# Where GpSimd waits at the entrances of the feed-forward parts and of the convolution mixer

## The reference

```python
def short_conv_mixer(h, norm_g, w_in, conv_w, w_out):
    xn = rms_norm_2(h, norm_g)
    proj = xn @ w_in
    gate_b = proj[..., :CONV_WIDTH]
    gate_c = proj[..., CONV_WIDTH:2 * CONV_WIDTH]
    u = proj[..., 2 * CONV_WIDTH:]
    y = gate_b * causal_dwconv(gate_c * u, conv_w)
    return y @ w_out

def conv_ffn_2(h, norm_g, w_up, conv_w, w_down):
    xn = rms_norm_2(h, norm_g)
    u = causal_dwconv(xn @ w_up, conv_w)
    g, val = u[..., :D_FF], u[..., D_FF:]
    return (jax.nn.silu(g) * val) @ w_down
```

## Time and profile before

| | |
|---|---|
| median of 3 runs | 1234.81 us (1234.18 to 1236.0) |
| profiled execution, its own time | 1238.09 us |
| profiled execution, span from first to last instruction | 1236.1 us |
| TensorE busy | 1224.3 us, 99% of the span |
| VectorE busy | 752.1 us, 61% |
| GpSimd busy | 712.6 us, 58% |
| ScalarE busy | 676.5 us, 55% |
| mean granted TensorE clock | 0.996 |

### The profile page before, as it was taken

One profiled execution on the slowest core, in us unless ns is written; L12 is line 12 of the kernel. 1 busy time (PEld: TensorE's weight loads), 2 busy tenths in 40 slices (PEclk: granted clock), 3 DMA queues, 4 the chain that ended last, 5 costly groups with the idle time before them and its releaser, 6 DMA issues.

```text
span 1236.1 us, 24028 instructions
## 1 busy us (share of the span) xinstructions
PE 1224.3 (99%) x8458; PEld 1090.7 (88%) x8458; DVE 752.1 (61%) x1660; ACT 676.5 (55%) x1226; POOL 712.6 (58%) x308
## 2 busy tenths in 40 slices
PE   8999999999999999999999999999999999999998
PEld 4788889877799999999988779999999989899998
DVE  5786667455641766655626654766667445766665
ACT  6343344454544755555755626666667556666663
POOL 5466553442168765557585305755565986755573
PEclk9999999999999999999999989999999999999999
DMA  9978552231135454456464203554554764555451
GB/s 338 374 251 301 202 160 84 84 104 52 52 115 177 154 204 183 174 197 210 130 205 137 86 1 104 204 177 179 201 206 122 221 201 124 188 201 191 168 214 57
DMA packets 58187, 208.08 MB, mean 168 GB/s; under 512 B 6640, under 2 KB 7808, under 8 KB 58112
## 3 DMA queue, kind: packets, MB, share of 16 engines
q1 hardware_dynamic: 57888, 206.56, 49.1%
q0 software_dynamic: 224, 0.52, 0.1%
HBM read 206.01 MB, written 1.05 MB: 168 GB/s over the span
## 4 chain that ended last, share of the span: by engine, by line
PE 93%; DVE 3%; DMA 1%; ACT 1%; POOL 1%; issue 1%; SPq 0%; DVEq 0%; ACTq 0%
PE ps L557 17%; PE ps L558 17%; PE ps L559 17%; PE ps L583 16%; PE ps L585 8%; PE ps L601 2%; PE ps L825 2%; PE ps L604 2%; PE ps L603 2%; PE ps L896 1%; PE ps L922 1%; PE ps L911 1%; DMA raw<-in_stream 1%; DMA X<-in_xc 1%; PE ps L1157 1%
## 5 line engine op out<-in xcount | busy, mean ns | idle before, releaser
L333 POOL TENSOR_TENSOR wlo<-raw,whi 128x1024 fp32r<-128x1024 f32 x287 | 696.1, 2439 | 495.4 <-ACT whi L1290 447.6
L1290 ACT ACTIVATE whi<-raw 128x1024 fp32r<-128x1024 f32 x338 | 353.1, 1054 | 96.1 <-PE ps L559 53.9
L557 PE MATMUL ps<-H,whi 128*128 128x256 f32 (+3 forms) x1144 | 340.0, 297 | 1.4 <-DVE H L1839 1.1
L558 PE MATMUL ps<-H,whi 128*128 128x256 f32 (+3 forms) x1144 | 330.0, 288 | 0.0
L559 PE MATMUL ps<-H,wlo 128*128 128x256 f32 (+3 forms) x1144 | 329.7, 288 | 0.0
L583 PE MATMUL ps<-H,whi 128*128 128x512 f32 x840 | 298.5, 398 | 0.0
L585 PE MATMUL ps<-H,wlo 128*128 128x256 f32 x840 | 235.9, 281 | 0.0
L557 PEld LDWEIGHTS ps<-H,whi 128*128 128x128 f32 (+1 forms) x1144 | 218.1, 191 | 15.3 <-issue 9.7
L558 PEld LDWEIGHTS ps<-H,whi 128*128 128x128 f32 (+1 forms) x1144 | 218.6, 191 | 2.5
L559 PEld LDWEIGHTS ps<-H,wlo 128*128 128x128 f32 (+1 forms) x1144 | 218.0, 191 | 2.5
L583 PEld LDWEIGHTS ps<-H,whi 128*128 128x128 f32 x840 | 158.0, 188 | 37.2
(11 more groups left out here) (340 smaller groups left out, 1539.7 us busy)
## 6 DMA issues: line engine op xcount, KB each, us to landing
raw<-in_stream SPq DMA_DIRECT2D x386, 512.0 KB, 4.1
X<-in_xc SPq DMA_DIRECT2D x4, 512.0 KB, 6.0
out_y<-X SPq DMA_DIRECT2D x8, 128.0 KB, 1.9
kx<-in_const SPq DMA_DIRECT2D x1, 512.0 KB, 8.2
params<-in_params SPq DMA_DIRECT2D x1, 344.0 KB, 6.6
kx<-in_const POOLq DMA_DIRECT2D x1, 256.0 KB, 4.4
k<-in_const POOLq DMA_DIRECT2D x1, 129.0 KB, 5.6
k<-in_const SPq DMA_DIRECT2D x1, 128.0 KB, 6.2
```

Of the source, the lines that this page charges most:

```text
L333: pool.tensor_tensor(wlo[:, slot, :], raw[:, rslot, :], whi[:, slot, :].bitcast(f32), ALU.subtract).then_inc(rest_done[0], 1)
L557: pe.matmul(out, lh, rh, start=start, stop=False, skip_group_check=True)
L558: pe.matmul(out, lh, rl, start=False, stop=False, skip_group_check=True)
L1290: act.activation(whi[:, s % RING, :], raw[:, r % RING, :], ACT.Copy).then_inc(hi_done, 1)
```

## The change

GpSimd's wait for the squares stands ahead of the rest of first+4 in place of first+2, in all four parts. The value that it waits for is the same.

```diff
-LATE_STARTS = {S_FFN1 + 2: 1, S_FFN2 + 2: 3, S_CONV + 2: 4, S_FFN3 + 2: 5}
+LATE_STARTS = {S_FFN1 + 4: 1, S_FFN2 + 4: 3, S_CONV + 4: 4, S_FFN3 + 4: 5}
```

## The result

| | before | after |
|---|---|---|
| median of the runs | 1234.49 us (4 runs, 1234.15 to 1236.0) | 1248.95 us (4 runs, 1248.42 to 1250.02) |
| ratio | | 1.0112, 95% interval 1.0092 to 1.0132 |
| profiled execution, its own time | 1238.09 us | 1250.02 us |
| its span | 1236.1 us | 1247.9 us |
| VectorE busy | 752.1 us | 770.0 us |

The change makes the kernel 14.5 us slower, where 11.2 were forecast; 1248.95 lies within the range of 1240.5 to 1254.5, and 0.95 above the 1244 to 1248 of the forecast's own case. Every engine's instructions stand in the same order as before, so all of it is waiting. Medians and ratios here leave out one slow execution of the run e1, 1970.62 us at a mean granted clock of 0.555 (with it e1's median would be 1240.17 us).

A forecast was written before the change was run, and what follows sets the result against it. TensorE was taken to bound the kernel, busy 99% of the span, its first block at each entrance following VectorE's chain. Stalls of 4.0, 3.6, 1.7 and 1.9 us sum to 11.2, added to 1234.8: 1246.0 us, range 1240.5 to 1254.5.

The forecast's parts named there:

- the forecast's own case: Whole kernel: stalls at the four entrances add 11.2 us, giving 1246.0 us, within 1244 to 1248; chance 0.42.
- Direction and mechanism: At the four entrances, GpSimd splits and VectorE's all-SBUF ops exclude each other and TensorE follows; slower, chance 0.90.
- Entrances 1, 2 and 4: VectorE's chains in FFN1, FFN2 and FFN3: moved splits make the last L2180 later by 4.0, 3.6 and 1.9 us.
- The price rule: VectorE's chain: a blocked all-SBUF op ends 0.29 us after the split's end; the next split ends 2.59 after the first.
- Entrance 3: Convolution mixer's chain: first L2180 passes, the split of first+3 holds the second L2180; 1.7 us late.
- given back: Behind the chain: GpSimd has two splits less to catch up, worth 0, bounds 0 and 0.8 us gained.
- Rival A: Entrances 1, 2 or both: TensorE's clock falls, 4 us per fall beyond 11.2, 1250 or 1254; chance 0.36.
- Rival B: Entrances: the lock costs once each, not twice; about 5.5 to 7 us in all, 1241; chance 0.12.
- Rivals C and D: Entrances: VectorE passes ahead (C, 1234.0 to 1235) or moved splits start behind the chain (D, 1234.8); chance 0.10 together.
- The moved hold costs nothing: GpSimd's hold ahead of first+4: costs nothing, as that block's high half comes behind the chain anyway.
- The earlier loads cost nothing: SP's loads into the two raw slots go out earlier; ScalarE's next splits still wait for TensorE, costed at nothing.

The follow-up runs named there:

- e1: Changed kernel with GpSimd's hold ahead of first+3 instead of first+4 in all four parts, one block later than before; 1239.97 us.
- e8: Changed kernel with the eight moved splits replaced by memsets of the same tile, which read nothing; 1236.84 us.
- e9: Changed kernel with the eight moved splits replaced by plain copies that read one tile; 1240.85 us.
- e4: Changed kernel with the hold at first+4 only in the convolution mixer and FFN3, back at first+2 in FFN1 and FFN2; 1238.97 us.
- e5: Changed kernel plus a GpSimd wait ahead of the split of first+6 until VectorE's third tap copy of the part is done; 1245.87 us.
- e2: Changed kernel with the four holds removed altogether; 1249.25 us.
- e3: Changed kernel with the hold at first+4 only in FFN1, back at first+2 in the other three parts; 1238.85 us.
- e6: Kernel before the change plus a GpSimd wait for the tap copy ahead of the split of first+6; 1235.06 us.
- e7: Changed kernel with each of the eight moved splits made in two ops of 512 columns with a wait between; 1247.36 us.

## Why the prediction was right, and where not

- **Direction and mechanism: right, shown.** Two splits of GpSimd moved into VectorE's chain shut its all-SBUF ops out one by one, and TensorE's first block follows the chain. e8 leaves the order of all work as it is and takes the reads of the eight ops away (they are also shorter, 0.96 us), and the entrances are back; e9 gives nearly the same op one read again, and two of them lose time again.
- **Entrances 1, 2 and 4: right.** 3.95, 3.50 and 1.88 for 4.0, 3.6 and 1.9. The chain's last L2180 is later by 3.92, 3.52, 2.21 and 1.90 us against its start, so TensorE follows it whole. The price rule (the op ends 0.29 behind the split's end, the next split ends 2.59 after) came from two rows that had ops of the chain's kind. Its second figure is a little high: rows 7 give 956.54 + 4.96 - 958.94 = 2.56, and after shows 2.54 and 2.51 at entrances 1 and 2. That is most of why 3.6 came out as 3.50.
- **Entrance 3: the order of a race was called wrong, and the term was mis-sized: 1.7, measured 2.18.** The forecast had the split of first+2 end as the first low half came, let that one pass, and had the second low half held. In after the second split starts at 953.77 (951.41 plus one of 2.36) and L2180 at 953.76, and it is VectorE that waits through the whole split, 2.69 us; the second low half then takes 0.47. One split costs one op either way; who is shut out changes the price by how much of the split is still ahead, here by half a microsecond. e4 has the same 2.70. In e1, where no split follows, the low half that comes as this one ends takes 0.49.
- **The term "given back": wrong in sign.** It was 0, with bounds of 0 and 0.8 us gained, because TensorE waited for no split behind the chain. That reading of TensorE's waits was correct, and it answered the wrong question. GpSimd's splits behind the entrance also changed their places in time against VectorE, and every round of VectorE's loop there has an all-SBUF op, the tap copy. The step that failed is "Given back: GpSimd has two splits less to catch up": it looked only at who waits for GpSimd, not at whom GpSimd shuts out. It measured 2.5 us, and e5, which only holds the split of first+6 until the copy is done, removes it. That the measured time still lies in the range of 1240.5 to 1254.5 is luck in this part: the range reached above the forecast's 1248 for the clock, not for this. The rows to see it by were in the trace of before: the tap copies of 0.52 and 1.01 us at 773.44 and 780.04, against 0.16 alone.
- **Rival A, the clock: it happened, at a small part of its price.** The clock fell at entrance 1 in every run with both splits moved there in full length (the change twice, e2, e3, e5), and not there in e1, e4, e6, e7, e8 and e9. Priced at 4 us per fall, it cost 0.0 to 0.3 where it lasted 3.4 us (first block of 9.24 to 9.54 against 5.29 + 3.91; the two ops alone are late by 1.76 + 2.15 = 3.91), and 1.2 in e2, where it lasted 6.8. This is worked out by subtraction; no run takes the fall away alone. What differs is whether the fall outlasts VectorE's chain: in after it is over at 419.3 and the chain at 420.6, and it costs nothing; in e2 it goes on to 419.8 where the chain ends at 418.6, and at entrance 2 of e7 to 766.7 where the chain ends at 765.5, and it costs 1.2 and 1.1. While TensorE waits for VectorE after each k, a slow clock is nearly free. The forecast took the 10.2 us of the old fall as its length, and it was a third of that; the old fall itself cost 4.5 us by the ledger, for a price of 5.1. The Trainium skill ("TensorE: Matmul & The Clock Gate", Part 1) says that idleness brings the slow clock back: at entrance 1 the traces agree each time, at entrance 2 in e2 and e7 alone. Of the 14.0 us in the ledger of after the clock carries less than one tenth of a microsecond by this subtraction; in executions without a trace it isn't known. 1248.95 is near A's 1250 for another reason, the tap copies.
- **Rival B (one exclusion per entrance): ruled out** by the two long ops at entrances 1 and 2. Its 1241 is near e1's 1240, in which one split moves.
- **Rivals C and D (no effect): ruled out** by the same rows.
- **The moved hold costs nothing: right.** GpSimd waits for ScalarE at first+4, and e2 without any hold is the same.
- **The earlier loads cost nothing: right** as far as the ledger shows: no block but these seven takes longer in both traces of the change, except the kernel's very first (0.8 and 0.7 us), some 350 us before the first entrance.

The prediction did not cite the rule that bears most on this. The Trainium skill ("SBUF — State Buffer", "SBUF: two separate sides") has the pair of ports that VectorE and GpSimd share as "an exclusive lock, not a bandwidth split", taken for a whole instruction by whichever comes first, among them VectorE's ops with two SBUF inputs, only against a GpSimd op that reads SBUF. The traces here agree: the waits to the end of the split, the 0.47 beside a fill (e8), the 0.86 and 1.25 beside an op that reads (e9). Who comes first can't be read off the starts to a hundredth: at entrance 3 the low half's record starts 0.01 us ahead, and it is the one that waits. The Trainium skill names VectorE's ops in a two-port mode there too, and its box on DMA counts a plain fp32 copy within SBUF among them. Of that the copies of 8 and 10 columns here, at up to 2.32 us for 0.16, are what the trace shows. Whoever had gone through VectorE's program with this rule would have listed L2107 next to L2180 and L2158.

## What to carry to other kernels

Where GpSimd reads SBUF beside a dense chain of VectorE, count how many of its ops start in the chain: each can cost the chain most of its own length, once (1.7 to 2.2 us for splits of 2.40 here), whoever waits for its result; an idle GpSimd can be the cheaper one. When work of such an engine is moved, list every all-SBUF op of VectorE, the tiny ones too, and see where each lies against the new times, behind the place of the change as well as in it. "Nobody waits for GpSimd here" isn't enough: its ops delay others without a wait that the profile could name, and it shows only as an op that takes longer than its kind's shortest.

## What the runs showed that was not expected

- A fill by GpSimd (0.96 us, nothing read) doesn't slow VectorE's all-SBUF ops at all (0.488 us at most at entrances 2 to 4), and a copy that reads one tile (1.05 us) shuts them out to its end, as a split with two reads does.
- An op of 0.16 us that moves 8 columns can take 2.32 us, fourteen times its time: the price is what is left of the other's length, not its own.
- A tie of 0.01 us (low half 953.76, split 953.77) went to GpSimd, in all five traces with both splits moved in full at entrance 3 (the change 2.69 and 2.68, e2 2.70, e4 2.70, e5 2.69).
- In code that no edit touches the clock falls in different places from run to run (7.6, 9.7, 230 to 232, 718 to 722, or nowhere), each from 3.41 to 13.65 us long, while the one at entrance 1 comes back each time that both splits are moved there in full. The change's own two traces differ so. Two profiled executions can therefore differ by a few us for no reason of the code; the ledger by blocks doesn't see it, unless the fall is in the block.
